# Taking the filler matmuls out of TensorE's waits in a two-block float32 network kernel

## The chip, the cores and the metric

One core of one Trainium2 chip runs the whole kernel in one launch. The metric is the time of one execution on the device in microseconds (us), lower is better. The kernel before was run three times: 1715.45, 1716.23 and 1717.67 us, median 1716.23 us.

## The reference

The input is `x`, 256 tokens of 1024 float32 values. Two blocks follow one another, all in float32:

```
first block:
  hn = rms_norm(x); proj = hn @ w_in                      # q,k,v,r,... and two gates
  ya = chunked gated linear attention (4 heads) @ w_br_gla
  yb = top-64 selected sparse attention (8 heads) @ w_br_att
  x += (sigmoid(gate_a)*ya + sigmoid(gate_b)*yb) @ w_out
  x += hierarchical MoE(rms_norm(x))                      # 32 experts, all computed, weighted
second block, 2 layers:
  h += 0.5*rms_norm(swiglu(rms_norm(h)))                  # width 2816
  h += rms_norm(mixer(rms_norm(h)))    # layer 0: RG-LRU recurrence, layer 1: forgetting attention, 16 heads
  h += 0.5*rms_norm(swiglu(rms_norm(h)))
```

Each `rms_norm` needs all of a token's values, so the result of the phase before must be complete, normalized and transposed before the next phase's first matmul can start. That puts a chain of work on the other engines between any two phases.

## The kernel before, in words

**Tiling.** Tokens are two tiles (`NT` = 2) of 128. Every weight matrix is streamed from memory in 512 KB pieces of 128x1024 float32 through a ring of six slots (`RING`). ScalarE rounds a piece to `w_hi` (L1115, L1170), VectorE computes the rest `w_lo` (L1531, L1536), and TensorE multiplies in three passes (`mm3`, L567 to L569: hi by hi, hi by lo, lo by hi), with 128x512 or 128x256 as the moving shape. Semaphores tie them together: `lo_done` tells TensorE that a piece is ready, `used` tells ScalarE that a slot is free.

**Order of the work.** It is written out by hand, one instruction stream for each engine. TensorE's is `norm(0)`, the input projection, attention parts, branches, `out`, `norm(1)`, router and `moe`, `norm(2)`, `ffn0`, `norm(3)`, the recurrent part `rgin` and `rgout`, `norm(4)`, `ffn1`, `norm(5)`, `kv`, `norm(6)`, `ffn2`, `norm(7)`, `q`, the second attention, `o`, `norm(8)`, `ffn3`. The bulk of each feed-forward is a loop on the engine (`pe.Fori`).

**norm(n).** For each of the two token tiles TensorE waits for `x_ready`, does 8 transposes of `x_res` into PSUM (L596), ScalarE writes `xT_hi` from them (L1124) and VectorE `xT_lo` (L1573). The next phase waits for all four groups (`xT_ready`).

**Fillers.** `keep_warm(n, bank)` (L577) issues n matmuls of 128x256 float32 on a table of constants (`con`), each of which stands as two instructions in the trace. They write a PSUM bank that nobody reads at that time, or, with `add_zeros`, add a product with a zero matrix to a bank in use. They stand ahead of a wait in TensorE's queue and wait for nothing themselves.


There are 312 of them: 134 in the nine norms (table `WARM`: ahead of token tile 0, ahead of tile 1, and after both), and 178 on 16 lines between L744 and L1089, among them 24 behind `qk_transposes(1)`, 11 at head 0 of the first attention, 5 and 8 around the combine transposes of the MoE, 77 in the recurrent output part, 6 at head 0 of the second attention.

**The first attention (L820 to L856)** goes head by head: logits of head h+2 (L816, L817), transposes of the probabilities of head h (L825), product with v of head h-1 (L832 to L834). `p_transposes(h)` waits until ScalarE (L1321) has written both parts of head h. The second attention has the same form (L1047, L1048, L1056, L1065 to L1067).

**The MoE's weights.** VectorE makes a table of expert weights (last step L1932), TensorE transposes it (L899), GpSimd sends it through memory (`comb_dram`) and gets it back broadcast over the partitions; VectorE waits for that before the expert loop.

**The recurrent output (four groups g).** TensorE transposes the gate (L945) once ScalarE's sigmoids (L1390) are done, transposes the next group's input (L923), which VectorE copies (L1979), does the output product of group g-1, then the small gate products (L935).

Of the kernel before, what the change touches and what calls it, by code (L numbers as in the profile page):

```python
# [25 lines left out]
P = 128  # L26
D = 1024
T = 256
# [23 lines left out]
CONST = {}  # L52
# [108 lines left out]
def two_blocks(nc, A, consts, out):  # L161
    with ExitStack() as ctx:
        def sb(name, cols, dt=F32, parts=P):
            return ctx.enter_context(nc.sbuf_tensor(name, [parts] + list(cols), dt))
# [4 lines left out]
        ps = ctx.enter_context(nc.psum_tensor("ps", [P, 8, 512], F32))  # L169
# [18 lines left out]
        con = sb("con", [CN])  # L188
# [40 lines left out]
        def sig(name):  # L229
            if name not in names:  # L230
                names[name] = sem(name)
            return names[name]

        def C(name, rows=P):
            lo, hi = CONST[name]
            return con[0:rows, lo:hi]

        ident = C("ident")
# [325 lines left out]
        def _(pe):  # L564
# [3 lines left out]
                pe.matmul(o, a_hi, b_lo, start=False, stop=False)  # L568
                return pe.matmul(o, a_lo, b_hi, start=False, stop=stop)  # L569

            zeros = con[:, CONST["adm"][0] + P:CONST["adm"][0] + 2 * P]

            def keep_warm(n, bank, add_zeros=False):


                for _ in range(n):
                    pe.matmul(ps[:, bank, 0:T], zeros if add_zeros else ident, con[:, 0:T], start=not add_zeros,  # L577
                              stop=not add_zeros)


            WARM = {0: (0, 0, 12), 1: (2, 2, 8), 2: (0, 2, 7), 3: (7, 4, 6), 4: (10, 5, 6), 5: (7, 4, 6), 6: (0, 0, 8),
                    7: (7, 4, 6), 8: (10, 5, 6)}

            def norm(n):

                for t in range(NT):

                    keep_warm(WARM[n][t], 7)
                    if n == 0:
                        pe.wait_ge(x_in, 16)  # L590
                    elif n != 6:
                        pe.wait_ge(x_ready, X_AT[n] - 1 + t)
                    v = x_res[:, t, :].rearrange("p (c k) -> p k c", k=KT)
                    for g in range(2):
                        for k in range(4):
                            m = pe.transpose(ps[:, 4 + 2 * t + g, k * P:(k + 1) * P], v[:, 4 * g + k, :], ident)  # L596
                        m.then_inc(norm_tr, 1)

                if n == 0:
                    pe.wait_ge(const_in, 16)  # L600
                elif n == 6:
                    pe.wait_ge(evicted, EV_RG + 6 + 2)
                keep_warm(WARM[n][2], 0)

            def spread(n, bank):

# [115 lines left out]
            def index_scores(t):  # L722
                keys = (t + 1) * P
                for g in range(4):
                    r = slice(32 * g, 32 * g + 32)
                    for u in range(2):
                        m = pe.matmul(ps[:, 4 + g, u * T:u * T + keys], qiT[r, u, t * P:(t + 1) * P], kiT[r, 0:keys],
                                      start=True, stop=True)
                m.then_inc(sig("idx_ps"), 1)
# [10 lines left out]
            for t in range(NT):  # L740
                m = pe.matmul(ps[:, 4, t * T:(t + 1) * T], alT[0:17, t * P:(t + 1) * P], s_(S_W2, 256, 17),
                              start=True, stop=True)
            m.then_inc(sig("z_ps"), 1)
            keep_warm(4, 2)  # L744
            pe.wait_ge(sig("z_read"), 2)
            pe.wait_ge(sig("tr1_ev"), 3)
            index_scores(1)
            i = gates(1, i)
            pe.wait_ge(evicted, 8)
            keep_warm(8, 0)  # L750
            pe.wait_ge(sig("relu_ok"), 1)
            index_scores(0)
            keep_warm(4, 0)

            pe.wait_ge(sig("relu_ok"), 2)
            pe.wait_ge(sig("la_ok"), 1)
# [32 lines left out]
            def qk_transposes(z):  # L789
                for a4 in range(4):  # L790
                    for t in range(NT):
                        c0 = (C_QB, C_KB)[z] + a4 * P
                        m = pe.transpose(ps[:, 2 * z + a4 // 2, (a4 % 2) * 256 + t * P:(a4 % 2) * 256 + (t + 1) * P],
                                         proj[:, t, c0:c0 + P], ident)
                m.then_inc(sig("tr2"), 1)

            qk_transposes(1)
            keep_warm(24, 0)

            pe.wait_ge(sig("og_ok"), 1)  # L800
            for t in range(NT):
# [1 line left out]
                    m = pe.transpose(ps[:, 4 + t, k * P:(k + 1) * P], proj[:, t, C_RA + k * P:C_RA + (k + 1) * P], ident)  # L803
            m.then_inc(sig("ogT_ps"), 1)
            qk_transposes(0)
            keep_warm(6, 7)
            pe.wait_ge(sig("ogT_ok"), 1)

            pe.wait_ge(sig("tr2_ev"), 2)
# [1 line left out]
            def qk(h):  # L811
                bk = 4 + h % 2 + 2 * ((h // 2) % 2)
                r = slice(64 * (h % 2), 64 * (h % 2) + 64)
                if h >= 4:
                    pe.wait_ge(sig("logit_read"), h - 3)
                pe.matmul(ps[:, bk, 0:P], qT[r, h // 2, 0:P], kT[r, h // 2, 0:P], start=True, stop=True)  # L816
                pe.matmul(ps[:, bk, P:P + T], qT[r, h // 2, P:T], kT[r, h // 2, 0:T], start=True, stop=True)\  # L817
                    .then_inc(sig("logit_ps"), 1)

            def p_transposes(h):  # L820
                pe.wait_ge(sig("prob_ok"), 2 * h + 2)
                if h >= 2:
                    pe.wait_ge(sig("pT_ok"), h - 1)
                for j in range(3):
                    m = pe.transpose(ps[:, h % 2, j * P:(j + 1) * P], prob[:, h % 4, j * P:(j + 1) * P], ident)  # L825
                m.then_inc(sig("pT_ps"), 1)

            def pv(h):
                pe.wait_ge(sig("pT_ok"), h + 1)
                v = slice(C_VB + 64 * h, C_VB + 64 * h + 64)  # L830
                o = slice(64 * h, 64 * h + 64)
                pe.matmul(ps[:, 2, o], pT[:, h % 2, 0:P], proj[:, 0, v], start=True, stop=True)  # L832
                pe.matmul(ps[:, 3, o], pT[:, h % 2, P:2 * P], proj[:, 0, v], start=True, stop=False)
                pe.matmul(ps[:, 3, o], pT[:, h % 2, 2 * P:3 * P], proj[:, 1, v], start=False, stop=True)\  # L834
                    .then_inc(sig("att_ps"), 1)
# [3 lines left out]
            for h in range(8):  # L839
                if h + 2 < 8:  # L840
                    qk(h + 2)
                if h == 0:
                    keep_warm(11, 0)
                p_transposes(h)
                if h:
                    pv(h - 1)
            pv(7)
            keep_warm(3, 5)
            pe.wait_ge(sig("oa_ok"), 1)
            for t in range(NT):  # L850
                for k in range(4):
                    m = pe.transpose(ps[:, t, k * P:(k + 1) * P], sq[:, t, k * P:(k + 1) * P], ident)
            m.then_inc(sig("oaT_ps"), 1)
            keep_warm(6, 5)
            pe.wait_ge(sig("oaT_ok"), 1)

            i = PLAN.start["branch"]
# [7 lines left out]
            for h in range(2):  # L865
                pe.wait_ge(sig("mixed_ok"), h + 1)
                for t in range(NT):
                    for k in range(4):
                        m = pe.transpose(ps[:, 4 * h + t, k * P:(k + 1) * P],
                                         xn[:, t, h * WID + k * P:h * WID + (k + 1) * P], ident)  # L870
                m.then_inc(sig("mixT_ps"), 1)
                keep_warm(5, 2)
            pe.wait_ge(sig("mixT_ok"), 2)
            i = PLAN.start["out"]
            for h in range(2):
# [17 lines left out]

            def combine_transposes():

                keep_warm(5, 1)
                pe.wait_ge(sig("comb_ok"), 1)
                for t in range(NT):
                    m = pe.transpose(ps[0:E_N, 2, t * P:(t + 1) * P], rt[18 + t][:, 0:E_N], ident)  # L899
                m.then_inc(sig("combT_ps"), 1)  # L900

                pe.wait_ge(norm_rb, RB_AT[1])
                pe.wait_ge(sig("combT_ok"), 1)
                for e in range(2):
                    m = pe.matmul(ps[:, 3, e * T:(e + 1) * T], C("first", E_N)[:, e * P:(e + 1) * P], combT[0:E_N, :],
                                  start=True, stop=True)
                m.then_inc(sig("comb01_ps"), 1)
                keep_warm(8, 1)
                pe.wait_ge(sig("comb01_ok"), 1)

            feed_forward("moe", E_N, logit_transposes, lambda: spread(1, 3), combine_transposes)
# [69 lines left out]
            pe.wait_ge(evicted, EV_RG + 6)  # L981
            for g in range(4):

                keep_warm((0, 14, 16, 18)[g], 0, g > 1)
                rg_gateT(g)
                if 0 < g < 3:
                    rg_transposes(g + 1)
                if g:
                    rg_out(g - 1)
                else:  # L990
                    keep_warm(13, 0)
                if g < 3:
                    rg_gates(g + 1)
            keep_warm(16, 0, True)
            rg_out(3)
            norm(4)
            pe.wait_ge(xT_ready, 20)
# [74 lines left out]
            for h in range(16):  # L1072
                if h + 2 < 16:
                    fqk(h + 2)
                if h == 0:
                    keep_warm(6, 0)
                fp_transposes(h)
                if h:
                    fpv(h - 1)
            fpv(15)  # L1080

            for h in range(2):
# [3 lines left out]
                        m = pe.transpose(ps[:, 4 + 2 * h + t, k * P:(k + 1) * P],  # L1086
                                         fo[:, t, h * WID + k * P:h * WID + (k + 1) * P], ident)
                m.then_inc(sig("foT_ps"), 1)
            keep_warm(6, 0)  # L1089
            pe.wait_ge(sig("foT_ok"), 2)  # L1090
            i = PLAN.start["o"]
            for h in range(2):
# [1055 lines left out]
```

## Time and profile before

| | |
|---|---|
| three runs | 1715.45, 1716.23, 1717.67 us |
| profiled execution, first to last instruction (span) | 1716.8 us |
| TensorE busy | 1653.9 us, 96% |
| VectorE / ScalarE busy | 1081.3 us, 63% / 800.3 us, 47% |
| mean granted TensorE clock | 0.991 of full speed |
| filler matmuls (L577) | 624 instructions, 144.2 us busy |

The page gives for the profiled execution its span alone; it lies 0.6 us above the median of the runs, and no other time stands around it. "Busy" of TensorE counts fillers like other matmuls, and ends of matmuls are modelled, so consecutive ones overlap in the rows: for the pace the distance between two starts is the better number. The granted clock is a share of 2.4 GHz, and 0.50 is 1.2 GHz.

### The profile page before, as it was taken

To read this page: it belongs to the slowest core of one execution; us is meant where nothing else is said; L and a number is where in the kernel's file an instruction comes from. 1 tells how busy PE (TensorE), PEld (TensorE's weight loads), DVE (VectorE), ACT (ScalarE), POOL (GpSimd) and SP (SyncE) were. 2 spreads that over 40 slices of the span, in tenths; PEclk is the share of its full clock that TensorE was granted. 3 is DMA by queue.
4 is the path that set the end of the run, shared out by engine and by line. 5 is a ranking of instruction groups with operands and counts; after the bars stand their busy time and mean duration, and the time that the engine had idled before them with its cause. 6 is when DMAs were issued, how large, how long until landed. Compare 5 with 4: busy or idle time off the path is not lost.

```text
span 1716.8 us, 27972 instructions
## 1 busy us (share of the span) xinstructions
PE 1653.9 (96%) x10510; PEld 1491.9 (87%) x10510; DVE 1081.3 (63%) x1921; ACT 800.3 (47%) x1175; POOL 35.4 (2%) x55
## 2 busy tenths in 40 slices
PE   7999999999999999999899999999899999999997
PEld 6877778899999899988787899988899988889997
DVE  4457655666666766666785766673866674376665
ACT  5465434344443544445675544452644454454442
POOL 4000000000000000000000000000000000000000
PEclk9999999999999999999999999999999999999999
DMA  9641142755555666635213566644566643246661
GB/s 245 232 147 53 50 147 88 265 186 186 187 186 168 185 188 186 184 122 184 67 44 106 171 187 185 189 126 135 167 201 184 190 126 112 74 125 186 188 184 63
DMA packets 258889, 266.10 MB, mean 155 GB/s; under 512 B 9192, under 2 KB 209084, under 8 KB 258448
## 3 DMA queue, kind: packets, MB, share of 16 engines
q1 hardware_dynamic: 255744, 255.87, 48.9%
q0 software_dynamic: 3088, 9.48, 2.1%
q8 instruction: 35, 0.57, 0.1%
q14 instruction: 22, 0.18, 0.0%
HBM read 264.21 MB, written 1.09 MB: 155 GB/s over the span
## 4 chain that ended last, share of the span: by engine, by line
PE 84%; DVE 10%; ACT 2%; issue 2%; DMA 2%; SPq 0%; POOL 0%; DVEq 0%; ACTq 0%
PE ps L567 26%; PE ps L568 25%; PE ps L569 25%; PE ps L577 2%; DVE xT_lo L1573 2%; DVE w_lo L1531 1%; DMA arena<-comb_dram 1%; DVE xn L1666 1%; PE ps L1047 1%; DMA con<-shape_constants_dram 1%; PE ps L935 1%; PE ps L1048 1%; DVE arena L1994 1%; PE ps L1056 0%; DVE arena L1750 0%
## 5 line engine op out<-in xcount | busy, mean ns | idle before, releaser
L567 PE MATMUL ps<-xT_hi,w_hi 128*128 128x256 f32 x2048 | 582.5, 284 | 10.8 <-DVE xT_lo L1573 6.0
L569 PE MATMUL ps<-xT_hi,w_lo 128*128 128x256 f32 x2048 | 581.4, 284 | 0.0
L568 PE MATMUL ps<-xT_lo,w_hi 128*128 128x256 f32 x2048 | 581.4, 284 | 0.0
L1170 ACT ACTIVATE w_hi<-raw 128x1024 fp32r<-128x1024 f32 x300 | 315.8, 1058 | 247.6 <-PE ps L569 242.0
L567 PEld LDWEIGHTS ps<-xT_hi,w_hi 128*128 128x128 f32 x2048 | 394.6, 193 | 18.4 <-DVE xT_lo L1573 8.4
L568 PEld LDWEIGHTS ps<-xT_lo,w_hi 128*128 128x128 f32 x2048 | 394.7, 193 | 4.2
L569 PEld LDWEIGHTS ps<-xT_hi,w_lo 128*128 128x128 f32 x2048 | 394.5, 193 | 0.0
L1536 DVE TENSOR_TENSOR w_lo<-raw,w_hi 128x1024 fp32r<-128x1024 f32 x300 | 357.4, 1219 | 8.6 <-DMA arena<-comb_dram 7.8
L1531 DVE TENSOR_TENSOR w_lo<-raw,w_hi 128x1024 fp32r<-128x1024 f32 (+4 forms) x189 | 222.8, 1210 | 113.7 <-ACT w_hi L1115 109.1
L1115 ACT ACTIVATE w_hi<-raw 128x1024 fp32r<-128x1024 f32 (+4 forms) x189 | 190.1, 1045 | 95.4 <-PE ps L569 85.1
L567 PE MATMUL ps<-w_hi,hid_hi 128*128 128x512 f32 x480 | 188.6, 393 | 4.4 <-DVE hid_lo L1606 3.1
L568 PE MATMUL ps<-w_lo,hid_hi 128*128 128x512 f32 x480 | 188.1, 392 | 0.0
L1165 ACT ACTIVATE sil<-sil 128x256 f32<-128x256 f32 x120 | 50.3, 419 | 294.5 <-DVE sil L1590 294.5
L569 PE MATMUL ps<-w_hi,hid_lo 128*128 128x512 f32 x480 | 186.8, 389 | 0.0
L567 PE MATMUL ps<-w_hi,xT_hi 128*128 128x512 f32 (+2 forms) x464 | 179.8, 388 | 4.6 <-DVE xT_lo L2025 1.8
L568 PE MATMUL ps<-w_lo,xT_hi 128*128 128x512 f32 (+2 forms) x464 | 177.7, 383 | 0.0
L569 PE MATMUL ps<-w_hi,xT_lo 128*128 128x512 f32 (+2 forms) x464 | 177.4, 382 | 0.0
L1590 DVE TENSOR_TENSOR sil<-ps,rb 128x256 f32<-128x256 f32 x120 | 50.9, 424 | 169.6 <-PE ps L569 153.9
L577 PE MATMUL ps<-con 128*128 128x256 f32 x624 | 144.2, 384 | 4.0 <-DMA con<-shape_constants_dram 4.0
L1596 DVE TENSOR_TENSOR hid<-sil,ps 128x256 f32<-128x256 f32 x120 | 50.5, 421 | 148.4 <-PE ps L569 147.4
L577 PEld LDWEIGHTS ps<-con 128*128 128x128 f32 x624 | 117.7, 193 | 21.4 <-DMA con<-shape_constants_dram 4.4
L567 PEld LDWEIGHTS ps<-w_hi,xT_hi 128*128 128x128 f32 x464 | 87.8, 189 | 24.9 <-DVE xT_lo L2025 2.2
(321 smaller groups left out, 1476.8 us busy)
## 6 DMA issues: line engine op xcount, KB each, us to landing
raw<-in_ffn_w_gate_dram SPq DMA_DIRECT2D x88, 512.0 KB
raw<-in_ffn_w_up_dram SPq DMA_DIRECT2D x88, 512.0 KB
raw<-in_ffn_w_down_dram SPq DMA_DIRECT2D x88, 512.0 KB
raw<-in_w_in_dram SPq DMA_DIRECT2D x40, 512.0 KB
raw<-in_w_gate_dram SPq DMA_DIRECT2D x32, 512.0 KB
raw<-in_w_up_dram SPq DMA_DIRECT2D x32, 512.0 KB
raw<-in_w_down_dram SPq DMA_DIRECT2D x32, 512.0 KB
raw<-in_rg_w_in_dram SPq DMA_DIRECT2D x16, 512.0 KB
```

The lines of the kernel that those rows point to most:

```text
L567: pe.matmul(o, a_hi, b_hi, start=start, stop=False)
L568: pe.matmul(o, a_hi, b_lo, start=False, stop=False)
L569: return pe.matmul(o, a_lo, b_hi, start=False, stop=stop)
L577: pe.matmul(ps[:, bank, 0:T], zeros if add_zeros else ident, con[:, 0:T], start=not add_zeros, stop=not add_zeros)
L1115: act.activation(w_hi[0:parts, i % RING, 0:cols], raw[0:parts, i % RING, 0:cols], ACT.Copy)\
L1165: act.activation(sil[:, par, :], sil[:, par, :], ACT.Silu).then_inc(silu_done, 1)
L1170: act.activation(w_hi[:, s, :], raw[:, s, :], ACT.Copy).then_inc(hi_done, 1)
L1531: dve.tensor_tensor(w_lo[0:parts, s, 0:cols], raw[0:parts, s, 0:cols], w_hi[0:parts, s, 0:cols].bitcast(F32), ALU.subtract).then_inc(lo_do ...
L1536: dve.tensor_tensor(w_lo[:, s, :], raw[:, s, :], w_hi[:, s, :].bitcast(F32), ALU.subtract)\
L1573: m = dve.scalar_tensor_tensor(xT_lo[o], ps[:, 4 + j, k * P:(k + 1) * P], gcol[:, n, 4 * g + k:4 * g + k + 1], xT_hi[o].bitcast(F32), ALU. ...
L1590: dve.tensor_tensor(sil[:, par, :], ps[:, 4 + par, 0:T], rb[:], ALU.mult).then_inc(gate_scaled, 1)
L1596: dve.tensor_tensor(hid[:, par, :], sil[:, par, :], ps[:, 6 + par, 0:T], ALU.mult).then_inc(hid_mul, 1)
```

## The change

The helper `keep_warm`, the table `WARM`, the slice `zeros` and every call are deleted. All waits, all other instructions and their order on every engine stay. The diff cut to its core (the other places are like the last ones):

```
-            zeros = con[:, CONST["adm"][0] + P:CONST["adm"][0] + 2 * P]
-
-            def keep_warm(n, bank, add_zeros=False):
-                for _ in range(n):
-                    pe.matmul(ps[:, bank, 0:T], zeros if add_zeros else ident, con[:, 0:T], start=not add_zeros,
-                              stop=not add_zeros)
-
-            WARM = {0: (0, 0, 12), 1: (2, 2, 8), 2: (0, 2, 7), 3: (7, 4, 6), 4: (10, 5, 6), 5: (7, 4, 6), 6: (0, 0, 8),
-                    7: (7, 4, 6), 8: (10, 5, 6)}
...
                 for t in range(NT):
-                    keep_warm(WARM[n][t], 7)
                     if n == 0:
                         pe.wait_ge(x_in, 16)
...
-                keep_warm(WARM[n][2], 0)
...
             qk_transposes(1)
-            keep_warm(24, 0)
...
                 if h + 2 < 8:
                     qk(h + 2)
-                if h == 0:
-                    keep_warm(11, 0)
                 p_transposes(h)
...
             def combine_transposes():
-                keep_warm(5, 1)
                 pe.wait_ge(sig("comb_ok"), 1)
...
-                keep_warm((0, 14, 16, 18)[g], 0, g > 1)
                 rg_gateT(g)
...
                 if g:
                     rg_out(g - 1)
-                else:
-                    keep_warm(13, 0)
                 if g < 3:
                     rg_gates(g + 1)
-            keep_warm(16, 0, True)
             rg_out(3)
```

## Rows read from the trace of the kernel before

**Rows 1.** The page: busy time by engine, clock in 40 slices, the fillers' group.

```profile
PE 1653.9 (96%) x10510; PEld 1491.9 (87%) x10510; DVE 1081.3 (63%) x1921; ACT 800.3 (47%) x1175; POOL 35.4 (2%) x55
...
PEclk9999999999999999999999999999999999999999
...
L577 PE MATMUL ps<-con 128*128 128x256 f32 x624 | 144.2, 384 | 4.0 <-DMA con<-shape_constants_dram 4.0
```

**Rows 2.** Busy time in chosen stretches; PEclk is the granted clock's share there.

```profile
core 0: us, PE busy (x) PEld busy (x) DVE busy (x) ACT busy (x) POOL busy (x), PEclk, DMA share, GB/s
...
842.80:844.66 1.86, 0.01 (x2) 0.01 (x1) 1.74 (x5) 1.84 (x2) 0.00 (x0) 1.00 0.00 0
...
134.60:136.80 2.20, 0.01 (x1) 0.01 (x1) 1.39 (x3) 1.02 (x1) 0.00 (x0) 1.00 0.00 0
137.60:144.30 6.70, 6.70 (x21) 5.63 (x20) 4.44 (x10) 3.84 (x5) 0.00 (x0) 0.50 0.01 2
...
182.00:185.30 3.30, 3.26 (x16) 3.27 (x17) 0.00 (x0) 1.09 (x2) 0.00 (x0) 0.50 0.00 0
...
312.30:318.40 6.10, 6.10 (x28) 6.10 (x29) 5.84 (x10) 3.25 (x4) 0.00 (x0) 0.50 0.77 266
...
1209.40:1212.70 3.30, 3.30 (x18) 3.30 (x17) 1.14 (x1) 3.29 (x5) 0.00 (x0) 0.50 0.17 65
1212.80:1220.00 7.20, 7.20 (x62) 7.20 (x61) 6.39 (x10) 5.27 (x6) 0.00 (x0) 1.00 0.72 218
```

**Rows 3.** Timeline of TensorE, 128x512 form, around the end of one low stretch.

```profile
142.25 0.63 PE L567 MATMUL ps<-w_hi,xT_hi 128*128 128x512 f32 x1
142.68 0.63 PE L568 MATMUL ps<-w_lo,xT_hi 128*128 128x512 f32 x1
...
145.07 0.39 PE L569 MATMUL ps<-w_hi,xT_lo 128*128 128x512 f32 x1
145.30 0.39 PE L567 MATMUL ps<-w_hi,xT_hi 128*128 128x512 f32 x1
```

**Rows 4.** Timeline of TensorE through `norm(3)`, without its other fillers.

```profile
760.29 3.18 PE L577 MATMUL ps<-con 128*128 128x256 f32 x14
764.05 1.16 PE L596 MATMUL ps<-con,x_res 128*128 128x128 f32 x8 [0.58 <-DVE x_res L1669]
...
767.47 1.16 PE L596 MATMUL ps<-con,x_res 128*128 128x128 f32 x8 [0.54 <-DVE x_res L1669]
...
771.61 0.50 PE L567 MATMUL ps<-w_hi,xT_hi 128*128 128x512 f32 x1 [0.39 <-DVE xT_lo L1573]
```

**Rows 5.** Timeline at head 0 of the first attention, ScalarE and TensorE.

```profile
190.74 0.49 ACT L1321 ACTIVATE xn<-xn,small 128x256 f32<-128x256 f32 x1
...
189.66 5.02 PE L577 MATMUL ps<-con 128*128 128x256 f32 x22
194.51 0.49 PE L825 MATMUL ps<-con,xn 128*128 128x128 f32 x3
```

**Rows 6.** Timeline at head 0 of the second attention.

```profile
1436.87 0.49 ACT L1321 ACTIVATE arena<-arena,small 128x256 f32<-128x256 f32 x1
...
1440.03 0.49 PE L1056 MATMUL ps<-con,arena 128*128 128x128 f32 x3
```

**Rows 7.** Timeline of the MoE's start: last step of the expert weights, transposes, resumption.

```profile
288.62 0.29 DVE L1932 TENSOR_TENSOR arena<-arena 128x32 f32<-128x32 f32 x2
...
290.59 0.38 PE L899 MATMUL ps<-con,arena 128*32 128x128 f32 x2
...
312.26 0.58 PE L567 MATMUL ps<-xT_hi,w_hi 128*128 128x256 f32 x1 [3.20 <-DVE w_lo L1536]
```

**Rows 8.** Timeline of group 2 of the recurrent output.

```profile
875.26 7.07 PE L577 MATMUL ps<-con 128*128 128x256 f32 x32
...
884.19 1.22 DVE L1979 COPY arena<-ps 84x1024 f32<-84x1024 f32 x1 [1.71 <-PE ps L923]
```

**Rows 9.** Busy time in the first attention's loop over heads.

```profile
194.50:207.50 13.00, 12.82 (x92) 10.51 (x90) 6.60 (x31) 9.58 (x32) 0.00 (x0) 1.00 0.01 1
```

More of the change, by code:

```diff
@@ L569, in mm3 @@
                 return pe.matmul(o, a_lo, b_hi, start=False, stop=stop)
[L571 to L582, printed above, removed]
             def norm(n):
                 for t in range(NT):
-                    keep_warm(WARM[n][t], 7)
                     if n == 0:
@@ L602, in norm @@
                     pe.wait_ge(evicted, EV_RG + 6 + 2)
-                keep_warm(WARM[n][2], 0)
             def spread(n, bank):
@@ L743, in _ @@
             m.then_inc(sig("z_ps"), 1)
-            keep_warm(4, 2)
             pe.wait_ge(sig("z_read"), 2)
@@ L749, in _ @@
             pe.wait_ge(evicted, 8)
-            keep_warm(8, 0)
             pe.wait_ge(sig("relu_ok"), 1)
             index_scores(0)
-            keep_warm(4, 0)
             pe.wait_ge(sig("relu_ok"), 2)
@@ L797, in _ @@
             qk_transposes(1)
-            keep_warm(24, 0)
             pe.wait_ge(sig("og_ok"), 1)
@@ L805, in _ @@
             qk_transposes(0)
-            keep_warm(6, 7)
             pe.wait_ge(sig("ogT_ok"), 1)
@@ L841, in _ @@
                     qk(h + 2)
-                if h == 0:
-                    keep_warm(11, 0)
                 p_transposes(h)
@@ L847, in _ @@
             pv(7)
-            keep_warm(3, 5)
             pe.wait_ge(sig("oa_ok"), 1)
@@ L853, in _ @@
             m.then_inc(sig("oaT_ps"), 1)
-            keep_warm(6, 5)
             pe.wait_ge(sig("oaT_ok"), 1)
@@ L871, in _ @@
                 m.then_inc(sig("mixT_ps"), 1)
-                keep_warm(5, 2)
             pe.wait_ge(sig("mixT_ok"), 2)
@@ L894, in combine_transposes @@
             def combine_transposes():
-                keep_warm(5, 1)
                 pe.wait_ge(sig("comb_ok"), 1)
@@ L907, in combine_transposes @@
                 m.then_inc(sig("comb01_ps"), 1)
-                keep_warm(8, 1)
                 pe.wait_ge(sig("comb01_ok"), 1)
@@ L982, in _ @@
             for g in range(4):
-                keep_warm((0, 14, 16, 18)[g], 0, g > 1)
                 rg_gateT(g)
@@ L989, in _ @@
                     rg_out(g - 1)
-                else:
-                    keep_warm(13, 0)
                 if g < 3:
                     rg_gates(g + 1)
-            keep_warm(16, 0, True)
             rg_out(3)
@@ L1074, in _ @@
                     fqk(h + 2)
-                if h == 0:
-                    keep_warm(6, 0)
                 fp_transposes(h)
@@ L1088, in _ @@
                 m.then_inc(sig("foT_ps"), 1)
-            keep_warm(6, 0)
             pe.wait_ge(sig("foT_ok"), 2)
```

## The prediction

> **What bounds the kernel now.** I read the page first, then the clock in chosen stretches, then timelines around the fillers. The page shows TensorE busy 96% of the span, of which the fillers are 144.2 us in 624 instructions; VectorE is at 63%, ScalarE at 47%, and every slice of the clock stands at nine tenths or more [rows 1]. So two things alternate. In the long phases TensorE streams three-pass matmuls back to back and sets the time. Between phases a chain on VectorE and ScalarE sets it, and TensorE would be idle without the fillers. Row group 4 shows one such joint: from 760.29 to 771.61 TensorE has 11.3 us, of which only two groups of eight transposes (1.16 us each) are real work; each time what ends the wait is VectorE (x_res L1669, xT_lo L1573), not TensorE [rows 4]. Taking fillers out of there makes nothing earlier as long as they end before the releaser, and they do: idle time of 0.58, 0.54 and 0.39 us is left behind them.
>
> **What an idle TensorE costs here.** The stretches show the granted clock at its two levels. After an idle stretch of 1.86 us (842.80 to 844.66) it stayed at 1.00, that is 2.4 GHz. After one of 2.20 us (134.60 to 136.80) it stood at 0.50, 1.2 GHz, for 6.7 us. The others I take from the same view: 3.3 us at 0.50 from 182.0, 6.1 us from 312.3 (after the 3.20 us wait of rows 7), 3.3 us from 1209.4; a fifth in the recurrent part is like these [rows 2, 7]. Matmuls ran densely in them, and the clock came back only after that. The price at the low level: 28 matmuls in 6.10 us are 218 ns each, 62 in 7.20 us are 116 ns each [rows 2]; in the wider form the starts are 0.43 us apart against 0.23 [rows 3]. Both ways a low microsecond loses 0.47 us. The mean of the four low stretches is (6.7 + 3.3 + 6.1 + 3.3)/4 = 4.9 us; the first holds some small work, so I take 4.5 us per restart: 4.5 x 0.47 = 2.1 us, with 3.3 x 0.47 = 1.6 and 6.7 x 0.47 = 3.1 as ends.
>
> **The change part by part.**
>
> *Fresh low restarts on the critical path.* Every place with a long filler group becomes idle time. Each filler instruction takes 7.07/32 = 0.22 us [rows 8], so their length is read off the counts in the code. Behind them dense matmuls start that bound the kernel: the branch products, the output projection, the router after norm(1), and the phases behind norms 2, 3, 4, 5, 7 and 8, the last group of the recurrent output, and the o projection: 11 restarts, none low today. 11 x 2.1 = 23.1 us (ends 11 x 1.6 = 17.6 and 11 x 3.1 = 34). No later wait of a feed-forward pays this back: TensorE is the busiest engine by far, 96% against 63% and 47% [rows 1], so the others have pieces ready for it.
>
> *Slower transposes inside the joints.* At the low clock 16 transposes took 3.26 us [rows 2], 0.20 each, against 8 in 1.16, 0.145 [rows 4]; a group of eight loses about 0.5 to 0.9. In a norm VectorE works through 16 pieces and has some lead, so I let 0.3 us through in norms 3, 4, 5, 7, 8 and all of 0.9 ahead of the output projection, where nothing covers it: 5 x 0.3 + 0.9 = 2.4 us (ends 0 and 5.4).
>
> *The first attention and small places.* The clock is low at 182.0 today already, but comes back at 185.3. Without fillers between the short groups I expect it low again at the loop's start: 2.1 us for the loop, 1.4 for the logits and transposes around it, and 1.2 us for the start of the kernel, the index scores and norm(6) together, where low or idle stretches exist today and get a bit longer: 4.7 us (ends 1 and 8).
>
> *The recurrent output.* Here VectorE and ScalarE set the pace, but VectorE's copy waits 1.71 us for TensorE's transposes [rows 8], so slow transposes reach it; against that fillers now overrun the releaser by about 1 us in group 2 and 1.6 in group 3. Net +0.1 us (ends -2.5 and +3).
>
> *What is gained.* Some groups run past the moment at which the wait would have ended. At head 0 of the first attention ScalarE is done at 190.74 + 0.49 = 191.2, and TensorE starts its transposes at 194.51: 3.2 us, and the loop behind it is TensorE-bound [rows 5, 9]. At head 0 of the second, 1436.87 + 0.49 = 1437.4 against 1440.03: 2.5 us [rows 6]. At the expert weights VectorE ends at 288.9, TensorE transposes at 290.59: 1.7 us [rows 7]. The two index-score fillers give 0.3 each. Last, a gain by the back door: VectorE can start the expert loop only when the table is back from memory, so the resumption at 312.26 hangs on that chain; TensorE, late by some 2 us from its low restart before it, will arrive close to that moment, the 3.20 us idle shrinks towards 1 us, and the clock does not fall there: 6.1 x 0.47 = 2.7 us [rows 2, 7]. The sum of gains is 3.2 + 2.5 + 1.7 + 0.6 + 2.7 = 10.7 us (ends 5 and 13).
>
> *Sum.* 23.1 + 2.4 + 4.7 + 0.1 - 10.7 = 19.6 us on the profiled execution's 1716.8 us; this span is 0.6 above the median of the runs, 1716.2, so I forecast 1716.2 + 19.6 = 1736 us. The mean granted clock should be about (0.991 x 1716.8 + 19.6 - 65)/1736 = 0.95, where 65 is half of some 60 further low us in dense work and some 70 low us in joints.
>
> **A rule weighed.** The stretch from 182.0 to 185.3 holds 16 instructions at 0.50, all of them transposes, and the next stretches are at 1.00 [rows 2]: transposes alone brought the clock back. The Trainium skill (TensorE: Matmul & The Clock Gate, Part 4: PE-mode transpose) says the reverse, that the full clock does not engage for transposes since they do not count as busy in the same way. The trace disagrees with it here. By the page the attention loop, with its transposes, would be slow to come back; that is the first rival below, to which I give a chance for another reason as well.
>
> **The rivals.**
>
> *The attention loop stays low throughout.* Its matmuls are small (64-wide, half the rows for the logits), and no row shows such work raising the clock. The loop takes 13.0 us at 1.00 with TensorE busy 12.82 [rows 9]; at half speed it takes up to 13 more, against the 2.1 counted: +11, 1747 us. Against it: the loop leaves TensorE no idle time.
>
> *Waits that transposes interrupt don't lower the clock.* The joints ahead of the branch products and the output projection have two waits of about 2.5 us each with eight transposes between; 1.86 us kept the clock, 2.20 lost it [rows 2]. If they keep it, 2 x 2.1 + 0.9 go: 1731 us.
>
> *Faster: the clock holds.* If it stays at 2.4 GHz in the waits as at 842.80 [rows 2], only the overruns count: 3.2 + 2.5 + 1.7 + 0.6 and 1 in the recurrent part are 9 us off, 1707 us. It decides from the place on where the clock is still at 1.00 behind an idle wait of 3 us and more; the five low stretches speak against it.
>
> *No change: the loss is absorbed.* If later waits on other engines take up TensorE's delay in most phases, gains and losses meet near 1716 us. Against it: most idle left today is inside the joints, behind which the phases start, not in front of slack.
>
> **How the numbers follow.** Forecast 0.61, loop low 0.17, interrupted waits 0.12, faster 0.06, no change 0.04. A change below 0.2% (3.4 us) can't be told from none: faster 0.06, same 0.04, slower 0.90. The range takes in the loop's rival and the ends of the restarts (17.6 for 23.1 with more gain, and 3.1 per restart in a few): 1725 to 1752 us.
>
> **What would show it.** Right: the clock at 0.50 behind each norm for 3 to 7 us, starts 0.43 or 0.21 us apart there; 194.51's transposes earlier against the logits by up to 3 us; xT_lo's end relative to the end of the phase before within 0.5 us of today; the expert loop's wait near 1 us with the clock at 1.00 behind it. Wrong: restarts at 1.00 after norms (faster), low stretches much longer than 7 us in dense phases (slower than the range), or idle time ahead of later waits that shrinks by what the restarts lost.

## The result and the profile after

The changed kernel takes 1745.45 us (median of 4 runs, 1744.1 to 1747.47) against 1716.95 us (4 runs) for the kernel before, run beside it: a ratio of 1.0165, 95% interval 1.0151 to 1.0178. It is slower by 28.5 us. The profiled execution has a span (first to last instruction) of 1745.6 us and took 1747.47 us as a run; its mean granted clock is 0.937, where it was 0.991.

The page of the changed kernel, the same lines as in [rows 1] (TensorE's waits are now real, and most slices of the clock with a joint in them lose a tenth or more):

```profile
PE 1571.6 (90%) x9886; PEld 1416.7 (81%) x9886; DVE 1081.9 (62%) x1921; ACT 799.9 (46%) x1175; POOL 35.4 (2%) x55
...
PEclk8998579999999999999888899989899989989999
```

VectorE and ScalarE did the same work in the same time as before; 624 instructions fewer on TensorE left it 82 us less busy, and the kernel 28.5 us later. The timeline of TensorE through `norm(3)` in the changed kernel answers to [rows 4]; the last column is the idle time and what ended it:

```profile
780.01 1.16 PE L582 MATMUL ps<-con,x_res 128*128 128x128 f32 x8 [3.60 <-DVE x_res L1635]
783.44 1.97 PE L582 MATMUL ps<-con,x_res 128*128 128x128 f32 x8 [2.27 <-DVE x_res L1635]
787.98 0.80 PE L567 MATMUL ps<-w_hi,xT_hi 128*128 128x512 f32 x1 [2.57 <-DVE xT_lo L1539]
```

And the busy time and clock (PEclk, before the DMA share) of stretches of the changed kernel, as in [rows 2] and [rows 9]:

```profile
776.41:780.01 3.60, 0.00 (x0) 0.00 (x0) 3.26 (x8) 1.46 (x5) 0.00 (x0) 1.00 0.54 201
781.17:783.44 2.27, 0.00 (x1) 0.01 (x1) 2.23 (x3) 2.27 (x9) 0.00 (x0) 0.50 0.01 4
788.00:791.20 3.20, 3.20 (x8) 2.52 (x9) 2.87 (x11) 3.18 (x4) 0.00 (x0) 0.50 0.01 3
196.00:219.70 23.70, 23.68 (x92) 19.47 (x92) 8.42 (x41) 10.12 (x36) 0.00 (x0) 0.50 0.00 1
225.70:231.40 5.70, 5.70 (x14) 4.45 (x15) 2.17 (x2) 0.63 (x2) 0.00 (x0) 0.50 0.51 177
231.60:250.60 19.00, 18.82 (x83) 15.24 (x82) 10.49 (x9) 6.00 (x6) 0.00 (x0) 1.00 0.51 168
```

The joint itself is hardly longer: 787.98 - 780.01 = 7.97 us from the first transposes to the restart, against 771.61 - 764.05 = 7.56 in [rows 4]. But the clock falls. It is still at 1.00 through the first idle wait of 3.60 us and the first transposes, which take 1.16 us as before; in the second wait it stands at 0.50, the second group of transposes takes 1.97 us instead of 1.16, and the dense matmuls behind the joint start low (3.3 us there). The fourth line is the new thing: the loop of the first attention, 92 instructions in 13.0 us at 1.00 in [rows 9], ran its 23.7 us at 0.50, and TensorE was busy 23.68 of them. The fifth and sixth show that it came back only 5.9 us into the first dense phase behind it, which starts at 225.66.

VectorE's 1921 instructions stand in the same order in both traces, so the difference between the starts of the same instruction tells where the 28.8 us of the two profiles arose:

| from where to where | predicted | difference in the traces |
|---|---|---|
| 11 dense restarts | 23.1 | 19.9 (1.5 to 2.5 each) |
| slower transposes in the joints | 2.4 | 2.6 |
| first attention's loop, logits and transposes around it | 3.5 | 10.6 |
| start, index scores, norm(6) | 1.2 | 1.9 + 2.3 + 1.0 = 5.2 |
| recurrent output | 0.1 | 0.3 |
| overruns gone: first attention, second, MoE, index scores | -8.0 | -2.0 - 2.5 - 2.6 |
| expert loop starts at full clock | -2.7 | -2.7 |
| sum | 19.6 | 28.8 |

The 1.9 us at the start come and go. Without its fillers TensorE starts the first phase 5.7 us earlier (15.25 for 20.93 us) and then runs out of pieces: in this execution it waits 3.09 us for `w_lo`, up to 29.49 us, and the clock is at 0.50 from 30.2 to 33.5. In the first experiment below, whose start is the same code, the wait is 2.11 us, the clock stays at 1.00, and VectorE is 0.8 us earlier than in the kernel before.

### The profile page after: what moved, and what is told of

It reads as the page before. It is cut to its first block, busy times and chain, and to the rows that moved or that the text cites. A ratio compares the mean times of both kernels' runs of the same rounds, so it can differ in the third digit from the quotient of the medians.

```text
span 1745.6 us, 26725 instructions
## 1 busy us (share of the span) xinstructions
PE 1571.6 (90%) x9886; PEld 1416.7 (81%) x9886; DVE 1081.9 (62%) x1921; ACT 799.9 (46%) x1175; POOL 35.4 (2%) x55
## 4 chain that ended last, share of the span: by engine, by line
PE 81%; DVE 12%; ACT 4%; issue 2%; DMA 1%; SPq 0%; DVEq 0%; ACTq 0%
PE ps L567 25%; PE ps L568 25%; PE ps L569 25%; DMA raw<-in_w_in_dram 1%; DVE xT_lo L1539 1%; DVE w_lo L1497 1%; DVE arena L1960 1%; DVE xn L1632 1%; PE ps L1016 1%; PE ps L1017 1%; ACT arena L1356 0%; ACT xT_hi L1090 0%; DVE x_res L1635 0%; PE ps L1025 0%; DVE arena L1980 0%
## 5 line engine op out<-in xcount | busy, mean ns | idle before, releaser
L567 PEld LDWEIGHTS ps<-xT_hi,w_hi 128*128 128x128 f32 x2048 | 399.0, 195 | 30.6 <-DVE xT_lo L1539 16.6
L568 PEld LDWEIGHTS ps<-xT_lo,w_hi 128*128 128x128 f32 x2048 | 399.1, 195 | 4.1
L567 PE MATMUL ps<-w_hi,xT_hi 128*128 128x512 f32 (+2 forms) x464 | 188.2, 406 | 28.7 <-DVE w_lo L1497 8.9
L568 PE MATMUL ps<-w_lo,xT_hi 128*128 128x512 f32 (+2 forms) x464 | 184.4, 397 | 0.0
L569 PE MATMUL ps<-w_hi,xT_lo 128*128 128x512 f32 (+2 forms) x464 | 183.5, 396 | 0.0
L1556 DVE TENSOR_TENSOR sil<-ps,rb 128x256 f32<-128x256 f32 x120 | 50.9, 424 | 174.4 <-PE ps L569 153.1
L567 PEld LDWEIGHTS ps<-w_hi,xT_hi 128*128 128x128 f32 x464 | 92.4, 199 | 51.4 <-DVE xT_lo L1991 7.9
L567 PEld LDWEIGHTS ps<-w_hi,hid_hi 128*128 128x128 f32 x480 | 91.2, 190 | 24.9 <-issue 5.3
L569 PEld LDWEIGHTS ps<-w_hi,hid_lo 128*128 128x128 f32 x480 | 90.7, 189 | 19.8
```

The source lines that it names most:

```text
L567: pe.matmul(o, a_hi, b_hi, start=start, stop=False)
L1556: dve.tensor_tensor(sil[:, par, :], ps[:, 4 + par, 0:T], rb[:], ALU.mult).then_inc(gate_scaled, 1)
```

## The experiments

Times of the kernel before beside each are 1716 to 1717 us.

**1. Eleven fillers put back at the loop's head, into the changed kernel.**

```
                 if h + 2 < 8:
                     qk(h + 2)
+                if h == 0:
+                    for _ in range(11):
+                        pe.matmul(ps[:, 0, 0:T], ident, con[:, 0:T], start=True, stop=True)
```

> The changed kernel with 11 filler matmuls put back at head 0 of the first attention, nothing else. In the changed kernel the loop over 8 heads took 23.7 us at the low clock against 13.0 before. Theory A (the low clock alone makes the loop slow; its own small matmuls do not raise it, dense work does): the 22 filler instructions start low, raise the clock after 3.4 to 6.8 us, end 5 to 7 us after the moment at which head 0 could start, and the loop then takes about 13 us: net 4 to 5.5 us faster than the changed kernel, 1740 to 1741.5 us. Theory B (the loop would have come back by itself within two or three heads, and the low clock there was chance of this one profile): the loop gains nothing on average and the fillers cost their 5 to 7 us: 1750 to 1752 us. Theory C (the clock falls again inside the loop): the low stretch returns within it, 1750 us or more.

Measured: 1742.21 us (1740.97 to 1743.93), ratio to before 1.0151 (1.0133 to 1.0168), 3.2 us under the changed kernel's median. Stretches of this kernel, and its timeline at the loop's head:

```profile
191.10:194.30 3.20, 3.20 (x9) 2.10 (x8) 2.81 (x14) 1.74 (x7) 0.00 (x0) 0.50 0.00 0
194.50:200.00 5.50, 5.50 (x31) 4.51 (x31) 1.27 (x6) 1.51 (x7) 0.00 (x0) 1.00 0.01 3
200.00:212.00 12.00, 11.18 (x80) 9.23 (x79) 6.51 (x30) 8.10 (x27) 0.00 (x0) 1.00 0.00 0
```

```profile
192.51 5.64 PE L824 MATMUL ps<-con 128*128 128x256 f32 x21
198.00 0.49 PE L805 MATMUL ps<-con,xn 128*128 128x128 f32 x3
```

The fillers take 5.5 us, the clock comes back within them (1.9 us behind the first, sooner than theory A had it), and the loop then runs at 1.00 to its end. Against the changed kernel, with the different starts of the two executions taken out, VectorE's part of the loop begins 3.6 us later and ends 5.6 earlier. That is theory A; B and C would have been slower than the changed kernel. The gain of the median, 3.2 us, is a little short of the 4 to 5.5 expected: in the traces some 2.9 us of what the loop gained are lost again at later joints, most of it up to the end of the expert loop. The intervals of the two ratios overlap, so the profile carries the verdict and not the times.

**2. Only the 122 fillers of norms 1 to 8.** The other calls are out and norm(0) has none:

```
-            WARM = {0: (0, 0, 12), 1: (2, 2, 8), ...
+            WARM = {0: (0, 0, 0), 1: (2, 2, 8), ...
...
-            keep_warm(24, 0)
+            pass
```

> The kernel before with only the fillers of norms 1 to 8 (122 of 312); the other 190 are gone. Theory A (each joint costs on its own: low clock on the dense work behind it): the norms' share of the changed kernel's loss, read from when VectorE's instructions come in the two traces, is 15.8 us, so this kernel stands at 1745.5 - 15.8 = 1730 us, at most 2.7 us more because TensorE now reaches the expert loop's wait early and idles there. Rival (what was lost at one joint is given back at the next, so that parts do not add up): further than 4 us from 1730, towards 1720 or 1740.

Measured: 1732.77 us (1730.41 to 1735.35), ratio 1.0098 (1.0078 to 1.0117). The parts add up: 1730 and at most 2.7 more was expected. By the medians the norms are worth 13 us of the 28.5, the rest of the fillers 16. The 2.7 us themselves did not come in the profiled execution (1730.41 us): there the expert loop starts at full clock.

**3. Transposes as fillers.**

```
-                    pe.matmul(ps[:, bank, 0:T], zeros if add_zeros else ident, con[:, 0:T], start=not add_zeros,
-                              stop=not add_zeros)
+                    if add_zeros:
+                        pe.matmul(ps[:, bank, 0:T], zeros, con[:, 0:T], start=False, stop=False)
+                    else:
+                        for _ in range(4):
+                            pe.transpose(ps[:, bank, 0:P], con[:, 0:P], ident)
```

> The kernel before with each filler matmul (except the 50 that add zeros to a bank in use) replaced by four 128x128 transposes of constants, of the same time in all. Theory A (transposes count like other work for the clock, as 16 of them at 182.0 to 185.3 us suggested): within 3 us of before, 1717 us, low stretches in the same places. Theory B (the Trainium skill, TensorE: Matmul & The Clock Gate, Part 4: PE-mode transpose: transposes do not count as busy in the same way): the clock falls in the joints as in the changed kernel, 1740 to 1746 us, less only what the 50 remaining matmul fillers save.

Measured: 1716.82 us (10 runs), ratio 0.9999 (0.9990 to 1.0009). Through norm(3) of this kernel the clock holds on transposes alone:

```profile
760.00:771.80 11.80, 10.38 (x88) 9.53 (x87) 11.03 (x33) 8.92 (x28) 0.00 (x0) 1.00 0.21 74
```

And they raise it too. At the kernel's start TensorE does 48 of these transposes, from 14.33 to 22.12 us and nothing else, behind a wait of 4.68 us:

```profile
14.00:19.60 5.60, 5.27 (x25) 5.27 (x26) 3.84 (x13) 4.66 (x8) 5.54 (x9) 0.50 1.15 124
19.70:21.00 1.30, 1.30 (x15) 1.30 (x14) 0.00 (x0) 0.18 (x1) 0.00 (x0) 1.00 1.41 127
```

Transposes of float32 did both as well as the filler matmuls. The rule weighed in the prediction does not hold here, now by a run and not by one stretch.

**4. The kernel before without the two MoE groups.**

```
             def combine_transposes():
-                keep_warm(5, 1)
                 pe.wait_ge(sig("comb_ok"), 1)
...
-                keep_warm(8, 1)
                 pe.wait_ge(sig("comb01_ok"), 1)
```

> The kernel before without the 5 and 8 fillers around the combine transposes alone. Theory A (what the prediction called a gain by the back door): the transposes start 1.7 us earlier, the restart behind them runs low and costs TensorE 2 us, but that delay lies in the idle time before the expert loop, which shrinks from 3.2 us to about 0 to 1, so that the clock holds and the 2.7 us of the low stretch at 312 go: 1717 - 1.7 - 2.7 = 1712.5 us. Rival B (the low restart costs as anywhere): 1717 - 1.7 + 2.1 = 1717.5 us. Rival C (the earlier start is all, and the expert loop's start falls low as before): 1715 us.

Measured: 1711.19 us (1710.21 to 1714.23), ratio 0.9968 (0.9954 to 0.9982): faster. The stretch behind the combine transposes and the one at the expert loop in this kernel, then the loop's first matmul:

```profile
292.90:302.90 10.00, 5.40 (x13) 4.28 (x14) 8.92 (x16) 7.15 (x9) 2.13 (x4) 0.50 0.81 265
311.50:320.00 8.50, 8.00 (x59) 7.60 (x59) 8.24 (x13) 3.80 (x6) 0.00 (x0) 1.00 0.68 238
```

```profile
312.03 0.39 PE L567 MATMUL ps<-xT_hi,w_hi 128*128 128x256 f32 x1 [0.50 <-DVE w_lo L1534]
```

The clock is low for 10 us earlier, and that costs nothing: TensorE comes late to a wait that was there anyway, the wait is 0.50 instead of the 3.20 us of [rows 7], and the clock stays at 1.00 behind it. Here fillers did harm, as the prediction said of this place. The median is 1.3 us lower than theory A had it; in the traces the MoE gives the 4.4 us expected, and a further 1.3 us come later, in the recurrent part, where no code was changed.

**5. Overruns trimmed.** Experiment 4 and:

```
-                    keep_warm(11, 0)
+                    keep_warm(4, 0)
...
-                if h == 0:
-                    keep_warm(6, 0)
                 fp_transposes(h)
...
-                keep_warm((0, 14, 16, 18)[g], 0, g > 1)
+                keep_warm((0, 14, 13, 14)[g], 0, g > 1)
...
-            WARM = {..., 1: (2, 2, 8), 2: (0, 2, 7), ...
+            WARM = {..., 1: (2, 0, 10), 2: (0, 0, 9), ...
```

> The kernel before with the fillers cut back only where the trace shows them past the end of the wait: both MoE groups out, 11 to 4 at the head of the first attention, 6 to 0 at that of the second, 16 and 18 to 13 and 14 in the recurrent output, the second group of norms 1 and 2 moved behind the transposes. Theory (overruns are paid in full where TensorE bounds what follows, and the clock holds): 1711.2 of the run without MoE fillers, less 3.2 and 2.5 at the two attentions and about 1 in the recurrent part: 1704.5 us, between 1702 and 1707. Rival (the two attention loops are paced by ScalarE and VectorE, so that an earlier start is waited away inside them): 1709 to 1711 us. Rival (4 fillers are too few and the loop falls low): 1714 us or more.

Measured: 1707.04 us (1706.06 to 1708.27), ratio 0.9943 (0.9929 to 0.9956). It is at the upper end of the range. In its trace the second attention brings 2.6 us for the 2.5 expected, the recurrent output 2.4 where about 1 was expected, and the first attention 2.6 instead of 3.2. Ahead of the first attention 1.3 us are lost: the low stretch that lasts 3.3 us in the kernel before [rows 2] lasts twice as long here, though the code ahead of it is the same:

```profile
181.30:188.00 6.70, 5.91 (x22) 5.46 (x23) 2.93 (x5) 3.26 (x4) 0.00 (x0) 0.50 0.00 1
```

**6. Trimmed, and filled where TensorE still sat idle.** Against experiment 5:

```
             index_scores(0)
-            keep_warm(4, 0)
+            keep_warm(8, 0)
...
             qk_transposes(1)
-            keep_warm(24, 0)
+            keep_warm(30, 0)
...
-                keep_warm((0, 14, 13, 14)[g], 0, g > 1)
+                keep_warm((0, 20, 13, 14)[g], 0, g > 1)
...
-                    keep_warm(13, 0)
+                    keep_warm(17, 0)
...
-            WARM = {..., 6: (0, 0, 8), ...
+            WARM = {..., 6: (0, 0, 15), ...
```

> The trimmed kernel with fillers added where the kernel before still sat idle ahead of a low stretch: 4 to 8 behind the index scores, 24 to 30 behind the first transposes of the attention, 13 to 17 and 14 to 20 in the recurrent output, 8 to 15 in norm(6). Theory (each low stretch costs 0.47 of its dense time): the stretches at 137, 182 and 1209 us go; 6.8 x 0.47 partly small work = 2, 3.3 x 0.47 = 1.5 and 1.6 us; the one at 858 lies beside work of VectorE and is worth 0.5: 5 us under the trimmed kernel, 1699.5 us. Rival (the transposes at 182 wait on VectorE and ScalarE, so only norm(6) pays): 2 us under it.

Measured: 1701.97 us (1701.21 to 1703.86), ratio 0.9910 (0.9895 to 0.9926): 15.3 us faster than the kernel before and 43 faster than the changed one. The places where the kernel before had low stretches, in this kernel:

```profile
130.00:150.00 20.00, 19.51 (x104) 16.09 (x103) 13.90 (x29) 10.63 (x12) 0.00 (x0) 1.00 0.17 51
180.00:190.00 10.00, 9.37 (x57) 7.57 (x58) 6.28 (x21) 5.64 (x13) 0.00 (x0) 1.00 0.01 2
835.00:850.00 15.00, 14.52 (x75) 12.14 (x74) 13.18 (x14) 11.06 (x16) 0.00 (x0) 1.00 0.33 93
1195.00:1208.00 13.00, 12.42 (x101) 12.04 (x100) 9.76 (x16) 11.33 (x14) 0.00 (x0) 1.00 0.63 193
```

All four are at 1.00. The gain over the trimmed kernel is 5.1 us. In the two traces 4.4 us are gained before 191 us, at the index scores and the attention's transposes. The rival, that these transposes hide behind VectorE, falls. But the profiled execution, the slowest of the four (1703.86 us), has two low stretches that the kernel before has not, each behind a short wait:

```profile
913.90:917.20 3.30, 3.30 (x10) 2.53 (x9) 0.82 (x1) 0.00 (x0) 0.00 (x0) 0.50 0.86 289
1218.89:1220.76 1.87, 0.00 (x0) 0.00 (x0) 1.82 (x4) 0.00 (x0) 0.00 (x0) 1.00 0.00 0
1221.10:1224.40 3.30, 3.30 (x18) 3.30 (x17) 3.23 (x6) 2.19 (x3) 0.00 (x0) 0.50 0.58 169
```

Each costs about 1.5 us; norm(6) brings 1.1. The waits ahead of them are 1.86 and 1.87 us. In [rows 2] a wait of 1.86 us kept the clock, so the length of the wait alone does not decide.

**7. Only the last filler group in norms 3, 4, 5, 7 and 8.**

```
-            WARM = {..., 3: (7, 4, 6), 4: (10, 5, 6), 5: (7, 4, 6), ..., 7: (7, 4, 6), 8: (10, 5, 6)}
+            WARM = {..., 3: (0, 0, 6), 4: (0, 0, 6), 5: (0, 0, 6), ..., 7: (0, 0, 6), 8: (0, 0, 6)}
```

> The kernel before without the first two filler groups of norms 3, 4, 5, 7 and 8 (55 fillers out), the last group of 6 ahead of the restart kept. Theory A (the clock falls in the first idle wait, and 2.8 us of fillers are not enough to bring it back before the restart): low at the restart but shorter than without any filler, since the fillers start the recovery 2.6 us earlier: per norm 2.1 in the changed kernel, here 0.5 to 1.5 us, 1717 + 5 x 1 = 1722 us. Theory B (work directly ahead of the restart is what counts): 1717 us, no low stretch behind these norms. Theory C (a fall costs the same however it is recovered): 1717 + 5 x 2.3 = 1728 us.

Measured: 1725.70 us (1724.85 to 1726.54), ratio 1.0050 (1.0034 to 1.0065), 8.4 us or 1.7 per norm: between A (5) and C (11). (The edit takes out 63 fillers, not the 55 of the expectation.) Stretches at norm(3) and norm(4) in this kernel, and TensorE's fillers in both:

```profile
763.00:769.60 6.60, 5.15 (x20) 4.48 (x21) 6.07 (x18) 5.50 (x20) 0.00 (x0) 0.50 0.01 1
771.70:780.00 8.30, 8.30 (x39) 6.83 (x38) 6.77 (x13) 6.60 (x8) 0.00 (x0) 1.00 0.49 143
951.80:960.00 8.20, 8.20 (x70) 8.17 (x69) 3.43 (x9) 2.06 (x3) 0.00 (x0) 1.00 0.46 127
```

```profile
766.42 1.97 PE L596 MATMUL ps<-con,x_res 128*128 128x128 f32 x8 [1.45 <-DVE x_res L1669]
768.18 3.54 PE L577 MATMUL ps<-con 128*128 128x256 f32 x12
...
948.09 4.04 PE L577 MATMUL ps<-con 128*128 128x256 f32 x12
951.77 0.47 PE L567 MATMUL ps<-xT_hi,w_hi 128*128 128x256 f32 x1
```

In all five norms the clock was low at the second transposes and back at 1.00 when the dense work started: the six fillers did raise it in time. The loss arises ahead of the restart. The 12 filler instructions run partly at the low clock, take 3.5 to 4.4 us instead of 2.6 (12 x 0.22), and reach past the moment at which `xT` is ready. In the traces norm(3) loses 0.9 us in all, the other four 1.3 to 1.7 each, together 7.0 us; another 1.0 comes from norm(6), where no code was changed. So B is right that no low stretch lies behind these norms and wrong that this costs nothing; A is near in its sum and wrong in its reason, since the restart is not low; C's 2.3 us for each fall is too much.

**8 and 9. Fillers of the attention's own kinds.** Half of the rows, as the logits, and 64 columns, as the product with v:

```
 # 8
+                        pe.matmul(ps[:, bank, 0:T], ident[0:64, :], con[0:64, 0:T], start=True, stop=True)
 # 9
+                        for _ in range(2):
+                            pe.matmul(ps[:, bank, 0:64], ident, con[:, 0:64], start=True, stop=True)
```

> The kernel before with fillers (but the 50 that add zeros) that use 64 of the 128 rows, as the attention's logits do, same shape and time otherwise. In the changed kernel the attention loop kept TensorE busy 23.68 of 23.70 us and the clock stayed low. Theory A (rows count: half-row work does too little for the clock): the fillers protect no joint, 1735 to 1745 us. Theory B (only time counts): 1717 us. Between the two: the clock survives in joints with continuous fillers but low stretches last longer, 1720 to 1728 us.

> The kernel before with each filler (but the 50 that add zeros) replaced by two matmuls of 128x64, the form of the attention's product with v, in which the loads of the stationary operand take most of the time (starts 0.11 us apart for 64 columns, so the groups take about as long as before). Theory A (streamed columns count, loads don't): joints fall low, 1735 to 1745 us. Theory B (only time counts): 1717 us, within 3.

Measured: half rows 1752.29 us (1751.87 to 1754.37), ratio 1.0208 (1.0185 to 1.0231), slower than no fillers at all; narrow 1730.04 us, spread from 1722.5 to 1748.09 over ten runs, ratio 1.0085 (1.0051 to 1.0120). The profiled runs took 1751.87 and 1747.35. Stretches of the half-row kernel, of which the first two hold fillers alone, then three of the narrow one, the first of them fillers alone:

```profile
14.40:24.90 10.50, 10.50 (x25) 7.79 (x25) 4.68 (x13) 5.32 (x9) 5.15 (x9) 0.50 1.26 112
196.90:206.40 9.50, 9.50 (x24) 6.97 (x22) 2.84 (x16) 1.97 (x8) 0.00 (x0) 0.50 0.00 0
184.50:240.20 55.70, 54.77 (x180) 43.42 (x180) 18.43 (x60) 17.57 (x48) 0.00 (x0) 0.50 0.01 2
770.00:800.00 30.00, 29.08 (x171) 24.92 (x170) 20.17 (x51) 15.91 (x37) 0.00 (x0) 1.00 0.33 104
```

```profile
198.60:208.20 9.60, 9.60 (x46) 9.58 (x46) 2.76 (x16) 1.98 (x8) 0.00 (x0) 0.50 0.01 2
186.10:237.00 50.90, 49.85 (x215) 44.85 (x215) 14.99 (x56) 15.63 (x47) 0.00 (x0) 0.50 0.00 1
770.00:800.00 30.00, 28.57 (x190) 25.89 (x189) 21.75 (x56) 17.16 (x38) 0.00 (x0) 1.00 0.24 71
```

Neither theory A nor B is right. Where the clock was high on entering a joint (norm(3) lies inside 770 to 800 us), both kinds kept it high. Where it was low on entering, they did not bring it back. The stretches with fillers alone show it without other work between: 10.50 and 9.50 us of half-row fillers and 9.60 us of narrow ones, TensorE busy all the time, and 0.50 throughout. The full-width fillers of experiment 1 stand at the same place, the head of the loop, and had the clock back 1.9 us behind the first of them. The same holds at the kernel's start. Behind the same 12 fillers of norm(0) the first dense matmul comes 7.2 us after the first filler in the kernel before and 7.8 with transposes, but 10.5 with half rows and 10.3 with narrow ones; in these two the dense matmuls start 0.43 us apart, at the low clock, and so 5 us of the loss in each profile lie ahead of everything else.

From 184.5 to 240.2 us the half-row kernel did its transposes, fillers, logits and products, 54.77 us busy, at 0.50; then dense matmuls ran low for 5.6 us more before the clock came back. That stretch also holds two groups of full-width transposes, 16 in a row from 185.43 and 8 from 232.90 us, with half-row fillers behind them, and the clock did not rise. In the narrow kernel it rose at 237.2 us, behind 8 transposes and 1.4 us of narrow fillers, before any dense work. So full-width work between small work brought the clock back in one case and not in others.

Fillers at the low clock also run twice as long and overrun their waits: at the head of the loop 9.59 us for 22 instructions, where the changed kernel waits 1.38 us. When the first attention ends, VectorE is 22.3 us behind the kernel before in the half-row kernel and 11.9 in the changed one; the norms give back a part of that difference. The ten times of the narrow kernel go with the clock: the two lowest, 1722.5 and 1723.35 us, have means of 0.988 and 0.991, the three highest, 1744.86 to 1748.09, of 0.967 to 0.972. The lowest are what the loss at the start alone would give (1716.2 + 5.4 = 1721.6 us, an estimate), so in some executions the attention may have kept the clock; only one of the longer ones was profiled.

**10. Without the 24, 6 and 11 fillers before the first attention.**

```
             qk_transposes(1)
-            keep_warm(24, 0)
...
-            keep_warm(6, 7)
...
-                if h == 0:
-                    keep_warm(11, 0)
```

> The kernel before without the 24, 6 and 11 fillers around the start of the first attention, nothing else. From the changed kernel's trace: the loop starts 2 to 3 us earlier (overrun gone) and takes 10.7 us more at the low clock, the transposes behind it 0.9 more; the fillers behind it (3 and 6) stay. Theory A (the loop's low clock is the whole cost and it is caused here): 1717 + 8 to 1717 + 10 = 1725 to 1727 us. Rival (the long loss in the changed kernel came from its surroundings, low from earlier gaps): less than 1721 us.

Measured: 1725.09 us (1724.21 to 1726.59), ratio 1.0048 (1.0030 to 1.0066), 8.9 us slower. The loop in this kernel:

```profile
189.20:219.70 30.50, 29.47 (x114) 23.96 (x111) 11.51 (x51) 11.11 (x40) 0.00 (x0) 0.50 0.00 1
```

The clock came back at 219.8 us, behind 3 full-width fillers and 8 transposes (4.3 us), ahead of the dense phase. These 41 fillers of 312 are worth a third of the whole change.

## Why the prediction was right, and which step of it was off

- *What bounds the kernel, and direction.* Right: VectorE ends the waits with or without fillers, a joint grows by 0.4 us, and the larger part of the loss lies in dense work behind the joints. The clock behind the norms was at 0.50 for 3.3 to 5.9 us, as said under "what would show it".
- *Fresh low restarts, 2.1 us each.* Right in kind and nearly in size: 11 restarts cost 19.9 us for 23.1. Experiment 2 shows that they add. The rival of interrupted waits (0.12) falls: the joint ahead of the output projection has waits of 2.56 and 2.50 us with eight transposes between, and the clock fell there.

```profile
256.20:258.66 2.46, 0.00 (x1) 0.01 (x1) 1.35 (x3) 2.46 (x4) 0.00 (x0) 0.50 0.00 0
258.70:262.20 3.50, 3.50 (x8) 2.77 (x9) 2.17 (x2) 0.47 (x1) 0.00 (x0) 0.50 0.09 14
```

- *Slower transposes.* 2.6 us for 2.4.
- *The first attention and small places, 4.7 us.* This is the mis-sized term. The first attention with its surroundings measured 10.6 us (9.2 in the loop) where 3.5 were counted, because I took for the loop the recovery of dense phases, 4.5 us. The rival that I gave 0.17, the loop low throughout, is what came: it gave 1747 us, measured are 1745.5. That it is so near is partly luck: the loop cost 7.1 us more than counted and not 11, and the index scores and the start made up most of the difference. Its reason, that such small work does not raise the clock, is shown for two kinds of it by experiments 8 and 9, and that the low clock is its whole cost by 1 and 10. The argument set against it, that the loop leaves TensorE no idle time, did not help: the clock had come back at 190.6 us and fell again at 194.0, just ahead of the loop, behind a wait of 2.57 us and in the middle of the logits. The index scores alone cost 2.3 us and norm(6) 1.0, where 1.2 us were set for these two and the start together.
- *Overruns gone.* Measured 7.1 for 8.0. At the first attention TensorE's first transposes come 3.2 us behind the logits (192.80 to 196.02) instead of 6.4 (188.15 to 194.51): 3.1 us gained, as predicted. The table has 2.0, because VectorE's next instruction already carries 1.1 us of the low clock at the loop's head; read at TensorE, the attention's term is larger by as much.
- *The gain by the back door at the expert loop, 2.7 us.* Right to the tenth in the traces, and seen alone in experiment 4. In the changed kernel the loop's first matmul follows without idle time worth a name:

```profile
329.03 0.39 PE L569 MATMUL ps<-w_hi,hid_lo 128*128 128x512 f32 x1
329.43 0.39 PE L567 MATMUL ps<-xT_hi,w_hi 128*128 128x256 f32 x1
```

- *The clock estimate.* 0.95 for a measured 0.937. In low time that is some 220 us for the changed kernel and 30 for the kernel before (estimates from mean clock and span), 190 more where 130 were counted. The attention's unbroken 37.5 us at 0.50, from 194.0 to 231.5, make up about half of the difference.
- *The 0.6 us between span and median.* The prediction read this as the distance of the two measures. A run's time is 1.9 us above its span (1747.47 and 1745.6 us for the profiled one here), so the profiled execution of the kernel before took some 1718.5 us, an estimate, and was one of its longer ones. The forecast of 1736 does not hang on it.
- *Not separated.* Which property of the small matmuls keeps them from raising the clock is open: half rows and narrow columns each failed in the same two places, and full-width transposes with no small work around them did not. Nor is it shown what decides after short waits: 1.86 us kept the clock in the kernel before and lost it in experiment 6.

## What to carry to other kernels

Work out for each wait of TensorE two numbers: how far the filler reaches past the releaser (paid in full where TensorE bounds what follows) and what runs behind the wait (dense work got its clock back after 3.3 to 5.9 us in the changed kernel and lost about 2 us; the loop of small matmuls did not get it back and ran at about half its speed to its end). Put fillers before the loops of small matmuls first, make them full-width, let them start directly behind the last real work (experiment 7: a group that starts after the clock has fallen runs long and overruns) and end just before the releaser, and leave out those ahead of a wait whose delay a later wait takes up: here that turned the kernel of 1717 us into one of 1702.

## What the runs showed of the hardware that I had not expected

- Keeping the clock and raising it take different work. Half-row and 64-column float32 matmuls kept 2.4 GHz through norm(3), but left the clock at 1.2 GHz through 10.50 and 9.60 us of unbroken fillers, and through 55.7 and 50.9 us of nearly unbroken work in which they and the attention's small matmuls were the most (experiments 8, 9).
- 128x128 transposes kept it too, 0.9999 of the time before, and 48 of them alone raised it at the kernel's start (experiment 3). The Trainium skill (TensorE: Matmul & The Clock Gate, Part 4: PE-mode transpose) says that they do not count in the same way; for float32 transposes these runs show otherwise.
- A low clock can be free: 10 us at 0.50 in experiment 4, and the kernel was 5.8 us faster.
- The length of a wait alone does not tell whether the clock falls: through 3.60 us ahead of norm(3)'s transposes it was still at 1.00 in the changed kernel, and behind 1.87 us in experiment 6 it fell.
